# A key projection that starts each chunk with its stacked tile, and sixteen cached pages turned at other half tiles

## The reference, cut to what matters

```python
kv = rmsnorm(x, kv_norm_w) @ w_kv                      # x: 320 tokens x 1024, w_kv: 1024 x 2048
k, v = jnp.split(kv, 2, axis=-1)
k = rmsnorm(k.reshape(B, T, MOBA_HEADS, MOBA_HD), k_norm_w)   # per head, 8 heads of 128
...
k_past = cache_k[pages].reshape(past, MOBA_HEADS, MOBA_HD)    # 8 sequences x 2 pages of 128 keys
scores = q . k_past + bias                             # then softmax, . v, gate, output projection
```

## Time and profile before

| | us |
|---|---|
| median of 3 runs | 507.18 (506.43 to 507.96) |
| the profiled execution | 506.81 |
| its span | 504.8 |
| TensorE busy | 491.4 (97%) |
| VectorE busy | 359.9 (71%) |
| ScalarE busy | 259.3 (51%) |
| GpSimd busy | 96.6 (19%) |

### The profile page before, as it was taken

The page is one execution under the profiler, slowest core; times in us unless marked ns, Lnnn a source line. Parts: engine busy times, 40 slices in busy tenths (PEclk is TensorE's granted clock), DMA queues, the critical chain, the costliest instruction groups (busy, mean ns, idle before and its releaser), DMA issues.

```text
span 504.8 us, 9913 instructions
## 1 busy us (share of the span) xinstructions
PE 491.4 (97%) x3689; PEld 424.8 (84%) x3689; DVE 359.9 (71%) x637; ACT 259.3 (51%) x532; POOL 96.6 (19%) x139
## 2 busy tenths in 40 slices
PE   7999999999999999999999999998798999999997
PEld 5989978899779977899899999976566778999885
DVE  3955539884799829894599978978766755776662
ACT  6735532574428633365553546835435655655630
POOL 0291004520072101820000152463002000000000
PEclk9999999999999999999999999999899999999999
DMA  9993969999799997999937979989987557684211
GB/s 265 350 348 104 275 244 319 382 354 241 274 342 387 242 268 277 367 322 227 265 113 270 343 223 258 207 206 215 237 295 229 200 185 244 225 310 145 84 52 52
DMA packets 86770, 125.54 MB, mean 249 GB/s; under 512 B 5491, under 2 KB 51524, under 8 KB 86596
## 3 DMA queue, kind: packets, MB, share of 16 engines
q1 hardware_dynamic: 85874, 124.63, 81.1%
q0 software_dynamic: 768, 0.28, 0.4%
q10 hardware_dynamic: 82, 0.02, 0.0%
HBM read 98.93 MB, written 27.57 MB: 251 GB/s over the span
## 4 chain that ended last, share of the span: by engine, by line
PE 92%; DVE 4%; DMA 1%; issue 1%; ACT 1%; SPq 0%; DVEq 0%; ACTq 0%
PE bank L928 46%; PE bank L925 19%; PE bank L909 7%; PE bank L1037 3%; PE bank L1099 2%; PE bank L1157 2%; PE bank L1051 1%; PE bank L984 1%; PE bank L1203 1%; DMA st<-in_x_prompt 1%; DVE w_lo L1565 1%; PE bank L1017 1%; PE bank L1018 1%; PE bank L1019 1%; PE bank L1005 1%
## 5 line engine op out<-in xcount | busy, mean ns | idle before, releaser
L1565 DVE TENSOR_TENSOR w_lo<-w_raw,w_hi 128x512 fp32r<-128x512 f32 x207 | 144.2, 735 | 61.8 <-ACT w_hi L1227 61.2
L1227 ACT ACTIVATE w_hi<-w_raw 128x512 fp32r<-128x512 f32 x208 | 118.8, 620 | 60.7 <-PE bank L928 35.0
L928 PE MATMUL bank<-xn_hi,w_hi 128*128 128x320 f32 x320 | 100.2, 317 | 0.8 <-ACT w_hi L1227 0.7
L928 PE MATMUL bank<-xn_hi,w_lo 128*128 128x320 f32 x320 | 97.8, 310 | 0.1
L928 PE MATMUL bank<-xn_lo,w_hi 128*128 128x320 f32 x320 | 97.7, 309 | 0.0
L925 PE MATMUL bank<-w_hi,xn_hi 128*128 128x512 f32 x160 | 64.5, 403 | 0.0
L928 PEld LDWEIGHTS bank<-xn_hi,w_hi 128*128 128x128 f32 x320 | 59.7, 188 | 5.0 <-issue 2.8
L925 PE MATMUL bank<-w_lo,xn_hi 128*128 128x512 f32 x160 | 62.5, 391 | 0.0
L925 PE MATMUL bank<-w_hi,xn_lo 128*128 128x512 f32 x160 | 62.4, 390 | 0.0
L928 PE MATMUL bank<-ym_hi,w_hi 128*128 128x320 f32 x192 | 61.0, 317 | 0.0
L928 PEld LDWEIGHTS bank<-xn_lo,w_hi 128*128 128x128 f32 x320 | 59.8, 188 | 0.4 <-DVE xn_lo L1614 0.2
(11 more groups left out here) (290 smaller groups left out, 784.6 us busy)
## 6 DMA issues: line engine op xcount, KB each, us to landing
w_raw<-in_ret_w_in SPq DMA_DIRECT2D x23, 1024.0 KB, 10.9
st<-in_state_ret SPq DMA_DIRECT2D x32, 512.0 KB, 8.6
out_ret_state_sample<-st SPq DMA_DIRECT2D x32, 512.0 KB, 4.7
w_raw<-in_ret_w_out SPq DMA_DIRECT2D x8, 1024.0 KB, 8.6
w_raw<-in_moba_w_in SPq DMA_DIRECT2D x8, 1024.0 KB, 6.6
w_raw<-in_w_kv SPq DMA_DIRECT2D x8, 1024.0 KB, 8.6
cache<-in_cache_v SPq DMA_DIRECT2D x16, 512.0 KB, 5.3
cache<-in_cache_k SPq DMA_DIRECT2D x48, 128.0 KB, 6.7
```

The lines of the kernel that those rows point to most:

```text
L928: mm = pe.matmul(bank[out][:, 0:T], w[:, wk, P * tile:P * tile + P], x[:, k, :], **flags)
L1227: act.activation(w_hi[:, c % 2, part], w_raw[:, c % RAW, part], ACT.Copy).then_inc(w_hi_done, 1)
L1565: dve.tensor_tensor(w_lo[:, c % 2, part], w_raw[:, c % RAW, part], w_hi[:, c % 2, part].bitcast(F32), ALU.subtract).then_inc(w_lo_done, 1)
```

## The change

The tile order of the key chunks becomes 2, 0, 1: the stacked tile first. `gaps`, the weight pieces and the page loads are then counted by position in the chunk, not by tile number. All places that named "the last tile" ask `tile_order` instead. The stores of the key rows and the KN steps follow the new order. The places of the side steps are new: pages 6 and 7 are turned before the first norming instead of during it, pages 10 and 11 before the first SE instead of behind it, pages 12 and 13 before the first copy of KX instead of behind both, and KX 0 and 1 stand one half tile later. The copies of KX, one bank by VectorE and one by ScalarE, are as they were.

```diff
-    return (2, 0, 1) if (kind, a, b) == ("mo", 1, 1) else tuple(range(TILES[kind]))
+    return (2, 0, 1) if kind == "mk" or (kind, a, b) == ("mo", 1, 1) else tuple(range(TILES[kind]))
...
-    g[5].append(("QT",))
-    for n, at in enumerate((0, 1, 4, 5, 7, 8, 9, 10, 12, 13, 15, 16, 18, 19)):
+    for n, at in enumerate((0, 1, 3, 4, 5, 5, 6, 8, 9, 10, 12, 13, 15, 16)):
         g[at].append(("KP", n + 2))
-    for q, at in enumerate((4, 10, 17, 22)):
-        g[at].insert(0, ("KS", q))
-    g[11].insert(0, ("SE", 0))
-    g[23].append(("SE", 1))
-    g[14].append(("KX", 0))
-    g[15].insert(0, ("KX", 1))
-    for n, at in enumerate((8, 10, 12, 20, 22, 24)):
+    g[4].append(("QT",))
+    g[4].append(("KS", 0))
+    for q, at in enumerate((9, 17, 21)):
+        g[at].insert(0, ("KS", q + 1))
+    for n, at in enumerate((8, 10, 11, 20, 22, 23)):
         g[at].append(("KN", n))
+    g[11].append(("SE", 0))
+    g[22].append(("SE", 1))
+    g[15].insert(0, ("KX", 0))
+    g[16].insert(0, ("KX", 1))
...
-                    for t, (c0, m) in enumerate(TOK):
-                        sp.wait_ge(rows_done, 3 * p + t + 1)
+                    for n, t in enumerate(tile_order("mk", p, 1)):
+                        m = TOK[t][1]
+                        sp.wait_ge(rows_done, 3 * p + n + 1)
```

More of the change, by code:

```diff
@@ L161, in chunk @@
         whole = c + 1 if paired and b == 0 else c
-        for i in tile_order(kind, a, b):
-            if i in starts:
-                steps.append(("WS", c + 1, starts[i]))
+        for pos, i in enumerate(tile_order(kind, a, b)):
+            if pos in starts:
+                steps.append(("WS", c + 1, starts[pos]))
             if whole == c and paired:
@@ L170, in chunk @@
                 fill(at, "TILE", whole, i)
-            mid, end = gaps[i] if i < len(gaps) and isinstance(gaps[i], tuple) else ([], gaps[i] if i < len(gaps) else [])
+            mid, end = gaps[pos] if pos < len(gaps) and isinstance(gaps[pos], tuple) else ([], gaps[pos] if pos < len(gaps) else [])
             cut = size // 2 if mid else 0
@@ L174, in chunk @@
                 steps.append(("MM", c, i, at, 0, cut))
-            if i in mids:
-                steps.append(("WS", c + 1, mids[i]))
+            if pos in mids:
+                steps.append(("WS", c + 1, mids[pos]))
             for s in mid:
@@ L629, in await_chunk_used @@
             else:
-                await_full(eng, *next((s[3], *s[:3]) for s in steps if s[:3] == ("TILE", c, TILES[chunks[c][0]] - 1)))
+                await_full(eng, *next((s[3], *s[:3]) for s in steps if s[:3] == ("TILE", c, tile_order(*chunks[c])[-1])))
         def chunk_source(c):
@@ L933, in project @@
                 if base + k1 < KT:
-                    if part == 0 and i == 2 and k1 == KT // 2:
+                    if part == 0 and i == tile_order(*chunks[c])[-1] and k1 == KT // 2:
                         mm.then_inc(pair_half, 1)
@@ L1487, in _ @@
                     n = step[1]
-                    m = TOK[n % 3][1]
-                    await_read(act, *tile_use("mk", n))
+                    t = tile_order("mk", 0, 0)[n % 3]
+                    m = TOK[t][1]
+                    await_read(act, *tile_use("mk", 3 * (n // 3) + t))
                     for d in range(4):
-                        ins = act.activation(rows[0:m, n % 3, P * d:P * d + P], rows[0:m, n % 3, P * d:P * d + P], ACT.Copy,
+                        ins = act.activation(rows[0:m, t, P * d:P * d + P], rows[0:m, t, P * d:P * d + P], ACT.Copy,
                                              scale=kss[0:m, n % 2, d:d + 1])
```

## The result

| | before | changed |
|---|---|---|
| median, first measurement | 506.93 us (506.43 to 507.96, 4 runs) | 510.32 us (509.01 to 510.5, 4 runs) |
| ratio of the two, 95% interval | | 1.0054 [1.0033, 1.0075] |
| profiled execution, its span | 506.81, 504.8 us | 509.01, 507.0 us |
| start of chunk 36 to start of chunk 41 | 63.4 us | 65.9 us |

The changed kernel was slower, where 505.3 us was forecast. Two more measurements, on two chips with twelve runs each, gave 1.0027 [0.9999, 1.0055] and 1.0011 [0.9979, 1.0043]. The three together, weighted by their intervals, give 1.0037 [1.0022, 1.0052], which is 1.9 us slower. The two repeats alone give 1.0020 [0.9999, 1.0041]: that the kernel is slower rests to a good part on the first measurement, and how much slower is not well known.

A forecast was written before the change was run, and what follows sets the result against it. TensorE, busy 97% of the span, was taken as the bound, so time could come only from its few gaps or its own work. (363.82 - 363.6) + 0.47 + 1.2 = 1.9 us off 506.81 gave 504.9, or 505.3 as median; range 502.4 to 507.5.

The forecast's parts named there:

- the four gaps named: TensorE's waits in the key projection: 1.54 us ahead of KS 1, 1.23 of KX 0, 2.44 of KX 1, 1.22 of KX 2.
- VectorE reaches chunk 39 at 357.5: VectorE's list: 19.7 us of work and 2.5 of waits from 335.4, reaching these pieces 1.6 us sooner than before.
- Chunk 39 issued at 347: SyncE's queue: pages 11 and 12 now stand ahead of this load, moving its issue from 342.37 by 2 x 2.3 us.
- It lands at 358.3: Landing of weight chunk 39, taken near page 12's row; 355.2, 358.2 and 359.8 were weighed.
- KX 1 is 5.3 after the landing: ScalarE's piece adds 0.62 us and VectorE's list ahead of the copy 4.68, putting KX 1 at 363.6.
- Six instead of eight matmuls, 0.47: Between KX 1 and KS 2, 6 matmuls lie instead of 8, saving 0.47 us of the former 4.0.
- the clock's 1.5 stays: From KX 1 to KS 2, the 1.5 us lost to the 0.50 clock remains, the gap ahead being no shorter.
- KS 2 keeps its 3.88: KS 2 still takes 3.88 us, 1.2 more than KS 0, with the stop inside it unchanged.
- KX 2 and KX 3 gain 1.2: The 1.22 us wait ahead of KX 2 and KX 3's 0.2 go; 0.2 is kept for KX 3, net 1.2.
- The stores are not felt: Key-row stores are down at about 373, TensorE finishes the second half's stacked tile at 372.9: nothing to pay.
- Rival 2: Chunk 39 lands late, perhaps at 362, with KX 1 at 367.3 and the kernel at 509.0, 1.8 slower; chance 0.12.
- rival 3: No measurable change: gap at KX 1 grows to 5.5 us or stores delay KX 2, 506.5 to 507; chance 0.2.

The follow-up runs named there:

- e0: The changed kernel, unedited, timed and profiled again as its first repeat; the two repeats together gave ratio 1.0020 [0.9999, 1.0041] against the kernel before.
- e8_before_long_rows: Kernel before with key pages read in rows of 4 KB instead of 1 KB pieces, for timing only; 0.57% less than the kernel before, median 506.45 us.
- e13_before_again: The kernel before, unedited, for a second profile; ratio 1 by construction, stage from chunk 36 to chunk 41 66.7 us instead of 63.4.
- e7: Changed kernel with key pages read in rows of 4 KB instead of 1 KB pieces, for timing only; 0.46% less than the kernel before, median 507.33 us.

## Why the prediction was wrong

The forecast was 505.3, the range 502.4 to 507.5, and "slower" had 0.10. The step that failed is the landing of chunk 39, taken at 358.3: it landed at 361.7, 3.4 us later, and put KX 1 at 367.0 instead of 363.6. A second term had been put at nothing without a reason, the wait for pages 7 and 8. In the first profile it held VectorE until 360.3, still ahead of the chunk's landing, so that the stop of 2.68 us it made on TensorE was paid out of the gap at KX 1. One row of the kernel before belongs to it, the last transfer of page 12, issued at 350.4 (KB, us from issue to landing):

```profile
cache<-in_cache_k SPq DMA_DIRECT2D x1, 128.0 KB, 9.3
```

Step by step:

- **What bounds the kernel**: right. The stage holds the loss, and the four gaps named are where it moved.
- **VectorE reaches chunk 39 at 357.5**: right where the pages were in time (357.7 in e0), 360.3 in the first profile, and 359.6 in the third, whose chunk 36 started 1.9 us later on the trace's clock than that of the kernel before. The list of its work was right; **that pages 7 and 8 would be there was assumed**. "Page 7 is turned at 341.4" was the step. In the changed kernel the first three transfers of page 7 took 5.4, 5.8 and 6.2 us, and the last, issued at 334.0, took 9.2, so that the page was complete at 343.2. The trace of the kernel before showed as much ahead of the forecast: its page 7 was complete at 341.7, after the 341.4 at which the forecast has it turned, and its page 8, whose last transfer was issued at 336.2 and took 9.1 us, at 345.3. A page is there when its last transfer is. This wait is new in two executions of three (3.16, 1.05, none).
- **KS 1's wait goes**: right. **KX 0 keeps 0.2**: right (none, 0.28, 0.38).
- **Chunk 39 issued at 347**: 348.6, 347.8 and 350.1, later by 0.8 to 3.1 (of the 3.1, 1.9 is the later start of chunk 36).
- **It lands at 358.3**: this is the term that turned the sign. It landed at 361.7, 359.2 and 363.8, 11.4 to 13.7 us after its issue. Of the three values weighed I took the one by page 12, on the ground that the same bytes must have passed by then. That value was itself misread: the 7.7 of the earlier trace rows is the median of four transfers, and the last of them took 9.3, so that page 12 was complete at 359.6 in the kernel before and not at 358.2. The ground failed too. In the changed kernel page 12 was complete at 357.0, and of page 13, issued behind the chunk, three transfers landed from 358.2 to 360.1, before the chunk, and the last at 363.9. So the bytes that share the engines with it are those issued after it too. "The same latency as before", 12.8, set at the measured issues, gives 361.4, 360.6 and 362.9, within 1.4 of each. That is partly luck: in the second profile of the kernel before the same chunk took 14.8 us.
- **KX 1 is 5.3 after the landing** (0.62 + 4.68): right to 0.1, 5.36 in all three profiles. The forecast had the whole losing from a landing after 360.2; two of three executions were past that.
- **Six instead of eight matmuls, 0.47; the clock's 1.5 stays**: right in the first profile, 3.57 from KX 1 to KS 2 where 3.54 was forecast; it was 4.00 and 3.94 in the other two, so there the 0.47 was not gained. A second stretch at 0.50, behind the stop at the stacked tile, was not counted; it lies ahead of KX 1 and cost nothing more.
- **KS 2 keeps its 3.88**: 4.18, 4.79, 2.69. Taking it for a constant was wrong: by the table above the end of its stop goes with a transfer, 2.3 to 2.6 us after it, and not with TensorE's arrival.
- **KX 2 and KX 3 gain 1.2**: 0.90 (21.12 us from chunk 39 to chunk 41, against 22.02). KX 2 has no wait, KX 3 waited 0.67 instead of 0.2.
- **The stores are not felt**: right, no engine waited for them in the stage.

Rival 2 described what happened (509.0 forecast for it, 510.3 measured first, 508.2 and 508.3 on the other chips). Its chance of 0.12 was too small because the landing was treated as one number with a best guess, when of the four values named one (359.8) lay 0.4 short of the break-even point and one (362, by the rival) past it. The range did not hold the first measurement; it left this rival out. The rival's path was right too: it has KX 1 at 367.3, measured 367.0. In e0 the chunk landed at 359.2, short of the break-even point, and the stage was still no shorter than in the first profile of the kernel before. One slip in the prediction's sums changes nothing: with the chunk at 359.8 its rival 3 has a gap ahead of KX 1 of 6.1 us by its own numbers (359.0 to 365.1), not 5.5. What is shown is thus why KX 1 was late; how much of the timed 0.37% it makes is not.

## What to carry to other kernels

In this kernel, with the DMA engines full, a step that releases a load is a step in the queue of all loads: moving it up moved other loads back, and the wait came back at a load that now stood behind. Count a load as there when its last transfer has landed, take its latency from loads of its own size under the same traffic, with their spread (11.4 to 14.8 us for chunk 39 in the five profiles of the two kernels), and put the break-even point beside the range of that latency before choosing a sign. For differences under 1% read the mechanism from the profile but the size from timings: the same kernel's stage differed by 3.3 us from one profiled execution to the next.

## What the runs showed of the hardware that was not expected

- A stop of 0.6 to 3.7 us inside a run of 128 small matmuls, ending 2.3 to 2.6 us after a transfer of the instruction queue, in ten of eighteen profiles.
- Gaps of 1.23 and 2.44 us a few us apart were followed by a clock of 0.50 in the kernel before, and the same gaps (1.23 and 2.43) by 1.00 in e8_before_long_rows. In e13_before_again 0.50 followed a gap of 2.00.
- Four transfers of one 512 KB page, issued within 2.5 us of each other, took 5.4, 5.8, 6.2 and 9.2 us to land. For pages 7 to 13 of the changed kernel's first profile the last transfer took 2.8 to 4.3 us longer than the third; with rows of 4 KB (e7, pages 7 to 12) it was 0.3 to 1.3.
- Reading 512 KB pages in rows of 4 KB instead of pieces of 1 KB made the kernel before 0.57% faster, though all of these loads run beside TensorE's work.
